# Six groups of extra TensorE products placed in waits of a three-block transformer kernel

## The reference, cut to what matters

```python
def reference(x, ...):
    x = first_block(x, ...)          # pool mixer, layer norm, dilated attention in 3 groups, layer norm
    x = second_block(x, ...)         # gated convolution, compressed/selected/window attention, gating unit
    return third_block(x, ...)       # gated recurrence in two directions, convolution, feed-forward part

def layer_norm(x, g, b):
    mu = jnp.mean(xf, axis=-1, keepdims=True)
    var = jnp.mean(jnp.square(xf - mu), axis=-1, keepdims=True)
    y = (xf - mu) * lax.rsqrt(var + LN_EPS) * g + b
...
def mixer_merge(...):                # in the third block
    u = cv_a * jax.nn.sigmoid(cv_b)
    u = jax.nn.silu(layernorm_3(dwconv1d(u, dw_w, dw_b), ln_w, ln_b))
```

## Time and profile before

| | |
|---|---|
| time before, median of 3 runs | 3283.52 us (3282.91 to 3283.69) |
| the profiled execution's own time | 3280.5 us |
| its span, first to last instruction | 3278.8 us |
| TensorE matmul busy | 3161.3 us, 96% of the span |
| VectorE, GpSimd, ScalarE busy | 50%, 47%, 32% |
| mean granted TensorE clock | 0.989 |

### The profile page before, as it was taken

One profiled execution on the slowest core, in us unless ns is written; L12 is line 12 of the kernel. 1 busy time (PEld: TensorE's weight loads), 2 busy tenths in 40 slices (PEclk: granted clock), 3 DMA queues, 4 the chain that ended last, 5 costly groups with the idle time before them and its releaser, 6 DMA issues. The chain is left out here.

```text
span 3278.8 us, 40501 instructions
## 1 busy us (share of the span) xinstructions
PE 3161.3 (96%) x14890; PEld 2434.6 (74%) x14890; DVE 1630.6 (50%) x2754; ACT 1064.3 (32%) x2039; POOL 1534.0 (47%) x875
## 2 busy tenths in 40 slices
PE   8999999999998999999999999899999999989998
PEld 7887897777765877777778777765556876868886
DVE  4761103433444054544531454427888897657731
ACT  2110202333334244444420123566666201331111
POOL 6665564343332534434456655710001554656664
PEclk9999999999999999999999999999999999999999
DMA  4233321322334322322234222311111221222221
GB/s 162 97 102 116 103 96 65 110 90 85 109 110 170 101 94 84 100 94 84 100 113 136 90 96 90 108 65 46 50 47 52 78 90 65 92 76 97 97 97 58
DMA packets 88471, 304.26 MB, mean 93 GB/s; under 512 B 9714, under 2 KB 11762, under 8 KB 88147
## 3 DMA queue, kind: packets, MB, share of 16 engines
q1 hardware_dynamic: 80352, 286.21, 25.8%
q10 hardware_dynamic: 7234, 12.98, 1.2%
q0 software_dynamic: 688, 2.49, 0.3%
HBM read 293.25 MB, written 5.77 MB: 91 GB/s over the span
## 5 line engine op out<-in xcount | busy, mean ns | idle before, releaser
L249 PE MATMUL psum<-arena_r,arena_r 128*128 128x512 f32 (+1 forms) x3096 | 1222.0, 395 | 40.4 <-DVEq L2848 13.2
L239 POOL TENSOR_SCALAR arena_r<-ring 128x1024 fp32r<-128x1024 f32 x431 | 460.5, 1068 | 1643.2 <-PE psum L251 1128.5
L250 PE MATMUL psum<-arena_r,arena_r 128*128 128x512 f32 (+1 forms) x3096 | 1197.1, 387 | 0.0
L251 PE MATMUL psum<-arena_r,ring_r 128*128 128x512 f32 (+1 forms) x3088 | 1194.3, 387 | 0.0
L241 POOL TENSOR_TENSOR ring_r<-ring,arena_r 128x1024 fp32r<-128x1024 f32 x431 | 1063.3, 2467 | 75.8 <-issue 39.3
L249 PEld LDWEIGHTS psum<-arena_r,arena_r 128*128 128x128 f32 x3096 | 584.7, 189 | 195.7 <-issue 65.2
L250 PEld LDWEIGHTS psum<-arena_r,arena_r 128*128 128x128 f32 x3096 | 585.1, 189 | 117.8 <-issue 4.6
L251 PEld LDWEIGHTS psum<-arena_r,ring_r 128*128 128x128 f32 x3088 | 583.5, 189 | 118.6
L876 DVE SCALAR_TENSOR_TENSOR arena<-arena,con,psum 128x512 f32<-128x512 f32 x64 | 47.8, 747 | 407.6 <-PE psum L801 407.6
L2155 PE MATMUL psum<-arena,ring 128*128 128x512 f32 x512 | 234.8, 603 | 14.4 <-ACT arena L2244 14.3
L2155 PEld LDWEIGHTS psum<-arena,ring 128*128 128x128 f32 x512 | 94.6, 194 | 114.2 <-issue 114.2
(11 more groups left out here) (415 smaller groups left out, 3895.1 us busy)
## 6 DMA issues: line engine op xcount, KB each, us to landing
ring<-in_weights SPq DMA_DIRECT2D x535, 512.0 KB, 3.3
gate_store<-arena ACTq DMA_DIRECT2D x14, 256.0 KB, 3.8
arena<-in_x_t SPq DMA_DIRECT2D x8, 256.0 KB, 5.7
arena<-arena ACTq DMA_DIRECT2D x16, 128.0 KB, 3.4
arena<-gate_store ACTq DMA_DIRECT2D x1, 2048.0 KB, 10.8
out_t<-arena SPq DMA_DIRECT2D x8, 256.0 KB, 2.2
arena<-gate_store ACTq DMA_DIRECT2D x1, 1536.0 KB, 7.4
arena<-in_w_ck POOLq DMA_DIRECT2D x1, 1024.0 KB, 10.8
```

The lines of the kernel that those rows point to most:

```text
L239: nc.gpsimd.tensor_scalar(hi_part(t), src, 1.0, 1.0, ALU.mult, ALU.mult)
L249: nc.tensor.matmul(out, w_hi, a_hi, start=start, stop=False)
L250: nc.tensor.matmul(out, w_hi, a_lo, start=False, stop=False)
L251: return nc.tensor.matmul(out, w_lo, a_hi, start=False, stop=stop)
```

## The change

A helper takes a PSUM bank, multiplies the table `mean_d` with the first 512 columns of the constants `con` n times into it, and frees the bank itself when the last product ends. Nobody reads the result. The helper is called at A with n = 4 into bank 0, at B with 4 into bank 1, at C with 3 into bank 3, at D with 2 into bank 0, at E with 5 into the bank of the tile that follows, and at F with 5 into bank 1. All other instruction lists are as before.

```diff
+        def stay_busy(pe, b, n):
+            bank_take(pe, b)
+            for i in range(n):
+                last = nc.tensor.matmul(psum[:, b], mean_d, con[:, 0:S], start=True, stop=True)
+            last.then_inc(bk_free[b], 1)
...
                 if then is not None:
                     mod_group(pe, t_mod + 8, c2, 0)
+                else:
+                    stay_busy(pe, 0, 4)
...
                 qk(0)
                 qk(1)
+                stay_busy(pe, 1, 4)
                 pe.wait_ge(dist_in, 32)
...
                 mod_group(pe, T0 + 4, c2, 5)
+                stay_busy(pe, 3, 3)
                 tiles_together(pe, [(at[job], bank_of[job]) for job in pre[:2]], h_hi, h_lo, h_lo_in)
...
                 seed_state(KT - 1)
+                stay_busy(pe, 0, 2)
                 pe.wait_ge(seeds, 1)
...
                 last.then_inc(pe_taps_done, 1)
+                stay_busy(pe, bank[order[-3]], 5)
                 mean(KT - 1).then_inc(mean_done, 1)
                 one(order[-3])
...
                 nc.tensor.matmul(psum[:, 7], mean_d, sq2[:, (KT - 1) % 2], start=False, stop=True).then_inc(sum_done, 1)
+                stay_busy(pe, 1, 5)
```

## The result

| | before | after |
|---|---|---|
| median of 13 runs each, us | 3281.99 (3278.77 to 3284.37) | 3274.91 (3271.39 to 3276.93) |
| profiled execution, us | 3280.5 | 3276.75 |
| its span, us | 3278.8 | 3275.0 |
| mean granted clock | 0.989 | 0.993 |

The ratio is 0.9979 [0.9971, 0.9986]: 7.1 us on the medians, where 9.3 were forecast. The change is faster, by about as much as a measurement of this kernel can tell.

The account below looks back on a forecast made before the run. TensorE, busy 3161.3 of 3278.8 us, was taken to bound the kernel. The terms 1.7 + 2.6 + 0.1 + 0.9 + 2.7 + 0 = 8.0, plus 1.3, gave 9.3 us: 3283.5 - 9.3 = 3274.2 us, range 3268.0 to 3280.8.

Parts of the forecast that it names:

- A: Wait of 4.83 us before 341.05; TensorE waits for nobody in the 4.42 us behind it, so all 1.7 us count.
- B: Wait of 5.12 us; transposes, `qk(2)` and part of a weight tile run slowly behind it; all 2.6 us count.
- C: Wait of 3.77 us before two tiles done by channel group; VectorE's low parts eat the gain: 0.1 us, bounds 0 and 0.2.
- D: Wait of 2.26 us at the first scores, where VectorE sets the pace: 0.9 us, bounds 0.4 and 1.7.
- E: Wait of 6.31 us before the last mean product and the sums of squares: 2.7 us, bounds 1.0 and 2.8.
- F: Wait of 13.24 us; 8.8 us stay empty behind five products, the clock falls again: gain 0, bounds +1.9 and -0.7.
- What the products cost: At all six waits: 0.88 us a product at the upper clock; all fit in the wait, so they cost nothing.
- Does the clock stay up: Idle stretches shrink to 0.5 to 1.9 us at A to E, counted as kept; at F the clock falls again.
- What moves besides: Waits without products: one of four recovered (2.2 us), one chance in two of a new fall (0.9): +1.3, ends -5.1 and +8.6.
- the products don't hold the clock: Rival: the gate counts something the products lack; nothing changes, 3283.5 us within 1.5; 6 in 100.
- low clock counts half wherever it lies: Rival: missing clock over waits and work counts, 18.6 us, giving 3264.9 us; 2 in 100.
- all four unfilled waits recovered: Four waits without products recover: 8.0 + 8.6 = 16.6 us, 3266.9; part of the rival "All of it arrives", 9 in 100.

Follow-up runs that it names:

- The narrow products: The change with products of 32 columns instead of 512 at all six places; 3281.64 us, 1.0001 [0.9992, 1.001] against before.
- the half with C: The change with products only at C, D and F (3, 2 and 5); 3281.13 us, 0.9997 [0.9988, 1.0006] against before.
- the half without: The change with products only at A, B and E (4, 4 and 5); 3273.96 us, 0.9974 [0.9964, 0.9983] against before.
- the double one: The change with twice the products at A to E (8, 8, 6, 4, 10), five at F; 3279.45 us, 0.9996 [0.9987, 1.0005] against before.
- F at fourteen: The change with 14 products at F in place of 5; 3271.21 us, 0.9967 [0.9955, 0.9979] against before.
- all waits filled: The change with 14 products at F and one to four in each of eight other waits; 3268.6 us, 0.9964 [0.9951, 0.9976] against before.
- three late products at F: The change with three products at F instead of five, held back until VectorE's second low part; 3271.47 us, 0.9972 [0.996, 0.9983] against before.
- the fastest one: The version with products in all waits, without those of head 5 and of the last head's scores; 3263.83 us, 0.9944 [0.9932, 0.9956] against before.
- The kernel without the last head's products: The version with products in all waits, without the four before the last head's scores alone; 3266.92 us, 0.995 [0.9937, 0.9964] against before.

## Why the prediction was right, and which step was wrong

The forecast was 3274.2 us, the median is 3274.9; 9.3 us of gain stood against 7.1. That the time came out within 0.7 us is in part luck. The forecast was taken off a median of three runs of before, 3283.5, and that of the thirteen is 3282.0. This 1.5 us made up for most of the 2.2 by which the gain fell short.

**What the products cost: right.** 4.45 us for E's five, 0.89 each, and the real work behind is on time at all six places. With double the number the cover is gone, and the overrun arrives in full at A, B and E; at C and D, where another engine sets the pace, it is made good.

**Does the clock stay up: right.** A to E at 1.00, F low. B and E, called unsafe with 1.6 and 1.9 us left empty, held with 1.49 and 1.99. The narrow products show that it takes full work.

**A, 1.7; B, 2.6; E, 2.7: right.** 1.6, 2.4 and 2.6 in after; 1.6, 2.4 and 2.6 in the kernel that has only them. Their sum, 6.6, lies in the interval of what this kernel gained (0.26% or 8.5 us of 3282.7, with 5.6 to 11.8); its profiled execution ends 6.4 us before that of before.

**C, 0.1: right.** VectorE's low parts set the pace; what is won or lost at the restart has vanished after seven channel groups, in after, in the half with C, in the half without and in the double one.

**D, 0.9: right within 0.2.** 0.7 in after, 0.7 with F at fourteen, 0.7 with all waits filled, 0.7 to 0.9 in the half. Without its products (only A, B and E) the lead is -3.72 ahead and -3.70 behind. Counted to 2459.40, past the waits at 2238 and 2450, the kernels with fourteen and with three late products at F, which have D's, gained 1.0 and 1.1 us, and the one without D's products 0.2, with the clock high behind 2238 and low behind 2450 in all three: 0.8 to 0.9 for D. The Trainium skill, "TensorE: Matmul & The Clock Gate", section "Why this matters for your kernels", asks for no idle gaps above about 3 us. The trace disagrees with the figure: the fall behind D came after 2.26 us, the one at 759 after a wait of 0.87.

**F, 0 with bounds of +1.9 and -0.7: the clock as forecast, but 0.9 lost in this execution, outside the lower bound.** Five products have no fixed price here: this kernel lost 0.9, the one with C, D and F 0.4 and the double one 0.1, and without them or with narrow ones it was at most 0.1. In the double kernel the real work starts at 2898.65, in after at 2896.37, and the low clock ends in both at about 2902:

```profile
2898.65:2902.14 3.49, 3.49 (x8) 0.50 0.00 0
```

Three and a half us of low work against 5.57. So how long before the end of a low stretch the work happens to restart sets its price. Whether the five products helped to place it there isn't shown.

**What moves besides, +1.3: the wrong step.** "I take one of the four as recovered [...] and one chance in two of a new fall". One did recover (2061, 1.6 us). But two waits fell anew, the one at 2238 was low for longer, and F too: -1.6, -0.8, -1.2 and -0.9, with the recovery -2.9 us in the profiled execution where +1.3 stood. On the medians this step is 7.1 - 7.3 = -0.2 us. The error was to draw a gain from the shift. By the prediction's own sign ("if two or more waits elsewhere change their sign") it was wrong here: three did, at 759 and 2878 to low and at 2060 to high. The time stayed near the forecast because the terms for A to E were right and a recovery made up for one of the new falls. Which short waits cost clock varies also where nothing was moved: the list of before, between B and C, lost 1.5 us more at 951 in the kernel with C, D and F than in before, and 26 runs of before alone spread from 3278.7 to 3284.7. The step should have had the value 0 and the same ends.

**The rivals.** That the products don't hold the clock is refuted by rows at 1.00. That low clock counts half wherever it lies would have given 3264.9. It fails at C, whose low stretch is free, and in the wait of F, where three products run low and 1.6 us is won all the same. The Trainium skill reckons in "TensorE: Matmul & The Clock Gate", section "HAM oscillation — how this bites in real kernels", that half of all low time is lost, and that is too high here: over the six waits and the work behind them it gives 18.6 us, where the traces show 7.5 at A to E and 1.7 at F once that wait is filled. Low time in an empty or a covered stretch costs nothing. The case of all four unfilled waits recovered (3266.9) didn't come by itself. With products in them and in the other waits the median fell to 3263.8.

**What stays open.** Why a wait of 0.87 us (759) takes the clock down in after and in the kernel with A, B and E, and not in before or the others, isn't settled; the work around it is the same in all. Nor are the single places shown by medians: those tell the change and the half with A, B and E from before, and both from the other half, the narrow and the double kernel; the terms of a place come from one execution of each kernel.

## What to carry to other kernels

Look for waits behind which the granted clock falls while the work that follows is TensorE's own; only there is the clock worth time, and the price is (1 - clock) times the length of that work. Fill such a wait with full-width products that end before the operand comes, as late as the wait allows (here 0.4 to 2.0 us ahead of it). The same number of narrow ones did nothing, and each us of overrun was lost in full at A, B and E. Where another engine sets the pace behind the wait leave it empty: what TensorE wins there goes into its next wait, which grows and may bring a fall of its own, as at the last head.

## What the runs showed that was not expected

A start that is earlier on TensorE can slow VectorE. In the kernel with all waits filled the work around the scores of head 5 stands elsewhere in time than in the fastest one, which has no products there: GpSimd's split of a weight tile begins 1.2 us earlier, and VectorE's subtractions, 0.42 us each, run into it. Timeline, VectorE and GpSimd:

```profile
2453.71 0.42 DVE L2442 TENSOR_TENSOR arena<-arena 128x256 f32<-128x256 f32 x1
2454.00 1.04 POOL L246 TENSOR_SCALAR arena_r<-ring 128x1024 fp32r<-128x1024 f32 x1 [10.44 <-DMA ring<-in_weights]
2454.04 1.27 DVE L2443 TENSOR_TENSOR arena<-arena 128x256 f32<-128x256 f32 x1
2455.19 2.35 POOL L248 TENSOR_TENSOR ring_r<-ring,arena_r 128x1024 fp32r<-128x1024 f32 x1 [0.15 <-issue]
2455.24 2.59 DVE L2444 TENSOR_TENSOR arena<-arena 128x256 f32<-128x256 f32 x1
```

In the fastest kernel (its line numbers are smaller by two) the last of these subtractions is over before GpSimd starts:

```profile
2454.22 0.42 DVE L2442 TENSOR_TENSOR arena<-arena 128x256 f32<-128x256 f32 x1
...
2455.18 1.04 POOL L246 TENSOR_SCALAR arena_r<-ring 128x1024 fp32r<-128x1024 f32 x1 [11.78 <-DMA ring<-in_weights]
```

The two rows of 1.27 and 2.59 us are 3.0 us longer than two of 0.42, and the lead that shrank by 2.1 us over this head fits. The kernel without the last head's products repeats both, 1.26 and 2.60 us and again 2.1 us of lead; without head 5's products neither is there. Products bring both about, then; that the long rows are what shrinks the lead is read from the traces and not tried by itself. The Trainium skill, "SBUF — State Buffer", section "SBUF: two separate sides", says that VectorE and GpSimd share one pair of ports under a lock held for a whole instruction, and that a VectorE operation with two SBUF inputs takes it against a GpSimd one that reads SBUF. The trace agrees: each slow subtraction ends 0.24 to 0.29 us after the GpSimd row beside it (2455.31 against 2455.04, 2457.83 against 2457.54).
